# A two-block transformer kernel: x in column halves around three weight chunks, and the first query products term by term

## What is computed

```python
def rmsnorm(x, g):
    y = xf * lax.rsqrt(jnp.mean(xf * xf, axis=-1, keepdims=True) + EPS)
    return (y * g.astype(jnp.float32)).astype(x.dtype)

def retention_layer(h, g_norm, w_in, gn_gain, w_out):
    proj = rmsnorm(h, g_norm) @ w_in
    q, k, v, gate = jnp.split(proj, [...], axis=-1)
    q = rotary(heads(q, RET_QK_DIM), pos)
    k = rotary(heads(k, RET_QK_DIM), pos) * (RET_QK_DIM ** -0.5)
    ...
```

## Time and profile before

| | |
|---|---|
| median of three runs | 870.59 us |
| profiled execution | 870.52 us |
| its span (first to last instruction) | 868.7 us |
| PE busy | 857.9 us (99%) |
| DVE busy | 604.3 us (70%) |
| ACT busy | 500.8 us (58%) |
| mean bandwidth of DMA | 178 GB/s |

### The profile page before, as it was taken

The page is one execution under the profiler, slowest core; times in us unless marked ns, Lnnn a source line. Parts: engine busy times, 40 slices in busy tenths (PEclk is TensorE's granted clock), DMA queues, the critical chain, the costliest instruction groups (busy, mean ns, idle before and its releaser), DMA issues.

```text
span 868.7 us, 12207 instructions
## 1 busy us (share of the span) xinstructions
PE 857.9 (99%) x4656; PEld 732.6 (84%) x4656; DVE 604.3 (70%) x1068; ACT 500.8 (58%) x873; POOL 36.1 (4%) x49
## 2 busy tenths in 40 slices
PE   9999999999999999999999999999999999999996
PEld 8998888888899999978888788888888887888885
DVE  5986666655767875769686566788459538777674
ACT  6434544446655675958778457654535447756530
POOL 0000000000010000000000001100020000000002
PEclk9999999999999999999999999999999999999999
DMA  8764544552584877443333457574764527534511
GB/s 317 284 213 175 194 147 144 206 193 98 195 266 144 278 239 222 147 146 97 118 125 98 146 194 224 187 263 137 261 205 156 172 97 245 191 123 168 172 71 49
DMA packets 86808, 154.36 MB, mean 178 GB/s; under 512 B 3744, under 2 KB 24352, under 8 KB 86752
## 3 DMA queue, kind: packets, MB, share of 16 engines
q1 hardware_dynamic: 85248, 149.19, 51.1%
q0 software_dynamic: 1360, 4.33, 1.8%
q10 hardware_dynamic: 144, 0.07, 0.0%
HBM read 152.53 MB, written 1.05 MB: 177 GB/s over the span
## 4 chain that ended last, share of the span: by engine, by line
PE 88%; DVE 7%; ACT 2%; issue 1%; DMA 1%; POOL 0%; SPq 0%; DVEq 0%; POOLq 0%; ACTq 0%
PE acc L2236 10%; PE acc L2238 10%; PE acc L2237 10%; PE acc L2210 9%; PE acc L2212 9%; PE acc L2211 9%; PE acc L2245 4%; PE acc L2247 4%; PE acc L2246 4%; PE acc L2251 3%; PE misc L2275 2%; PE misc L2405 2%; DVE wboth L1453 2%; PE acc L2252 2%; PE acc L2265 1%
## 5 line engine op out<-in xcount | busy, mean ns | idle before, releaser
L1453 DVE TENSOR_TENSOR wboth<-raw,wboth 128x1024 fp32r<-128x1024 f32 (+1 forms) x280 | 326.2, 1213 | 55.9 <-ACT wboth L970 54.3
L970 ACT ACTIVATE wboth<-raw 128x1024 fp32r<-128x1024 f32 (+1 forms) x280 | 279.0, 1051 | 121.1 <-PE acc L2238 73.6
L2236 PE MATMUL acc<-wboth,xhiA 128*128 128x512 f32 x272 | 107.8, 396 | 0.0
L2238 PE MATMUL acc<-wboth,xloA 128*128 128x512 f32 x272 | 106.1, 390 | 0.0
L2237 PE MATMUL acc<-wboth,xhiA 128*128 128x512 f32 x272 | 106.0, 390 | 0.0
L2210 PE MATMUL acc<-wboth,xhiA 128*128 128x512 f32 x240 | 93.9, 391 | 0.0
L2212 PE MATMUL acc<-wboth,xloA 128*128 128x512 f32 x240 | 93.5, 389 | 0.0
L2211 PE MATMUL acc<-wboth,xhiA 128*128 128x512 f32 x240 | 93.4, 389 | 0.0
L2251 PE MATMUL acc<-xC,wboth 128*128 128x512 f32 x192 | 68.6, 398 | 0.0
L2236 PEld LDWEIGHTS acc<-wboth,xhiA 128*128 128x128 f32 x272 | 51.1, 188 | 11.5 <-issue 1.2
L2238 PEld LDWEIGHTS acc<-wboth,xloA 128*128 128x128 f32 x272 | 51.0, 188 | 10.8
(11 more groups left out here) (329 smaller groups left out, 1736.7 us busy)
## 6 DMA issues: line engine op xcount, KB each, us to landing
raw<-in_w_in_dram SPq DMA_DIRECT2D x36, 1024.0 KB, 5.3
raw<-in_ret_w_in_dram SPq DMA_DIRECT2D x22, 1024.0 KB, 5.2
raw<-in_nsa_w_in_dram SPq DMA_DIRECT2D x16, 1024.0 KB, 5.4
raw<-in_kv_w_dram SPq DMA_DIRECT2D x12, 1024.0 KB, 5.8
raw<-in_ret_w_out_dram SPq DMA_DIRECT2D x8, 1024.0 KB, 5.0
raw<-in_ple_w_gate_dram SPq DMA_DIRECT2D x8, 1024.0 KB, 5.1
raw<-in_nsa_w_out_dram SPq DMA_DIRECT2D x8, 1024.0 KB, 5.1
raw<-in_cmp_w_k_dram SPq DMA_DIRECT2D x4, 1024.0 KB, 5.5
```

Of the source, the lines that this page charges most:

```text
L970: nc.scalar.activation(to_hi, src, ACT.Copy).then_inc(hi_done, 1)
L1453: nc.vector.tensor_tensor(to_lo, src, to_hi.bitcast(F32), ALU.subtract).then_inc(lo_done, 1)
L2236: nc.tensor.matmul(o, xh, hi[:, j, off:off + cols], start=start, stop=False)
L2238: ins = nc.tensor.matmul(o, xl, hi[:, j, off:off + cols], start=False, stop=stop)
```

## The change

x is loaded as four DMAs: columns 0 to 511 of both tiles first, then chunks 0, 1 and 2, then columns 512 to 1023 of both tiles, then the other chunks. Accordingly PE transposes only k-tiles 0 to 3 at first; k-tiles 4 and 5 are transposed after the products of chunks 0 and 1, k-tiles 6 and 7 after those of chunk 2. ACT may take each of the first four tiles as soon as it is done (semaphore `first_columns_made`). The products of `ret_q0` are issued by term: for a k-tile the four of hi by xhi, then four of hi by xlo, then four of lo by xhi, each set with a wait of its own. There are three products of ones ahead of x's transposes where there were four, and none behind them where there was one. DVE makes chunk 5's remainder between its two `norm_stats`, where it made it after the roots were spread.

```diff
-WARM = (4, 1)
+WARM = 3
...
-    norm("ret")
+    m("norm", "ret", 0)
+    r("ret_q0", [0, 1])
+    m("norm", "ret", 1)
+    r("ret_q0", [2])
+    m("norm", "ret", 2)
+    m("norm", "ret", 3)
+    r("ret_q0", [3, 4])
     for i in range(2):
-        r(f"ret_q{i}")
         if i == 0:
             m("roots")
+        else:
+            r(f"ret_q{i}")
         r(f"ret_k{i}")
...
         @block.sync
             for m in range(MT):
-                sp.dma_start(h[:, m], w["x"][0, m * P:m * P + P]).then_inc(x_in[m], 16)
+                sp.dma_start(h[:, m, 0:HALF], w["x"][0, m * P:m * P + P, 0:HALF]).then_inc(x_in[m], 16)
             for c, (key, src, ks, width, *_) in enumerate(plan.chunks):
...
+                if c == 2:
+                    for m in range(MT):
+                        sp.dma_start(h[:, m, HALF:], w["x"][0, m * P:m * P + P, HALF:]).then_inc(x_rest_in[m], 16)
...
             def first_norm_hi():
                 for k in range(KD):
-                    misc_wait(act, "norm", "ret", k % 4)
-                    if k >= 4:
-
-                        act.wait_ge(operand_ready, xt_no["norm", "ret", k - 4] + 1)
+                    if k < 4:
+                        act.wait_ge(first_columns_made, k + 1)
+                    else:
+                        misc_wait(act, "norm", "ret", k % 4)
...
             first_norm_lo()
             norm_stats("ret", 0)
+            split_until(len(FIRST_CUTS))
             asked = norm_stats("ret", 1)
...
+            def first_queries(i, first, last):
...
+                pe.wait_ge(hi_done, plan.pieces_upto[c] + 1)
+                for j, k in enumerate(ks):
...
+                    pe.wait_ge(operand_hi_done, xt_no["norm", "ret", k] + 1)
+                    for f, (o, wh, wl) in enumerate(slices):
+                        nc.tensor.matmul(o, wh, xh, start=first and j == 0 and f % 2 == 0, stop=False,
+                                         skip_group_check=True)
+                    pe.wait_ge(operand_ready, xt_no["norm", "ret", k] + 1)
+                    for o, wh, wl in slices:
+                        nc.tensor.matmul(o, wh, xl, start=False, stop=False, skip_group_check=True)
+                    if j == 0:
+                        pe.wait_ge(lo_done, plan.pieces_upto[c + 1])
+                    for o, wh, wl in slices:
+                        ins = nc.tensor.matmul(o, wl, xh, start=False, stop=last and j == len(ks) - 1,
+                                               skip_group_check=True)
+                ins.then_inc(chunk_used, 1)
...
                         if j == 0:
                             pe.wait_ge(head_in, 16)
-                            for m, ks in ((0, (0, 4, 1, 5, 2)), (1, (0, 4)), (0, (6, 3, 7)), (1, (1, 5, 2, 6, 3, 7))):
+                            for m, ks in ((0, (0, 1, 2)), (1, (0, 1)), (0, (3,)), (1, (2, 3))):
                                 pe.wait_ge(x_in[m], 16)
                                 for k in ks:
...
+                        elif j < 3:
+                            for k in (2 * j + 2, 2 * j + 3):
+
+                                pe.wait_ge(operand_ready, xt_no["norm", "ret", k - 4] + 1)
+                                for m in range(MT):
+                                    pe.wait_ge(x_rest_in[m], 16)
+                                    ins = first_transpose(m, k)
+                                ins.then_inc(misc_full[k % 4], 1)
...
-                    if step[1] == ("norm", "ret", 3):
-                        ones_products(WARM[1])
```

More of the change, by code:

```diff
@@ L668, in build @@
         x_in = [sem(f"x_in{i}") for i in range(MT)]
+        x_rest_in = [sem(f"x_rest_in{i}") for i in range(MT)]
+        first_columns_made = sem("first_columns_made")
         const_in = sem("const_in")
@@ L1043, in _ @@
                 act.wait_ge(x_in[m], 16)
+                act.wait_ge(x_rest_in[m], 16)
                 for nb in range(2):
@@ L2170, in last_rows @@
                 return nc.tensor.matmul(o, xl, hi[:, j, at], start=False, stop=stop)
+            def first_queries(i, first, last):
+                blk = plan.blocks["ret_q0"]
+                key, _, ks, width, *_ = blk["chunks"][i]
+                c = plan.chunk_no[key]
+                ps = pair("ret_q0")
+                n = len(ks) * width
+                hi = whi[plan.slot[c]][:, 0:n].rearrange("p (k n) -> p k n", n=width)
+                lo = wlo[plan.slot[c]][:, 0:n].rearrange("p (k n) -> p k n", n=width)
+                pe.wait_ge(hi_done, plan.pieces_upto[c] + 1)
+                for j, k in enumerate(ks):
+                    xh, xl = operand(blk, k, 0, T)
+                    slices = [(ps[f // 2][:, (f % 2) * T:(f % 2) * T + T], hi[:, j, f * P:f * P + P],
+                               lo[:, j, f * P:f * P + P]) for f in range(4)]
+                    pe.wait_ge(operand_hi_done, xt_no["norm", "ret", k] + 1)
[11 more added lines that the diff above has]
+                ins.then_inc(chunk_used, 1)
             def chunk(name, i, first, last, part=None, rows=False):
+                if name == "ret_q0":
+                    first_queries(i, first, last)
+                    return
                 blk = plan.blocks[name]
@@ L2276, in transposes, with first_transpose @@
                 return ins
+            def first_transpose(m, k):
+                return nc.tensor.transpose(first_columns(k)[:, m * P:m * P + P], h[:, m, k * P:k * P + P], ident)
             def misc(name):
@@ L2290, in misc @@
                             pe.wait_ge(head_in, 16)
-                            for m, ks in ((0, (0, 4, 1, 5, 2)), (1, (0, 4)), (0, (6, 3, 7)), (1, (1, 5, 2, 6, 3, 7))):
+                            for m, ks in ((0, (0, 1, 2)), (1, (0, 1)), (0, (3,)), (1, (2, 3))):
                                 pe.wait_ge(x_in[m], 16)
                                 for k in ks:
[L2294 to L2297, removed]
+                                    ins = first_transpose(m, k)
+                                    if m:
+                                        ins.then_inc(first_columns_made, 1)
+                        elif j < 3:
[3 more added lines that the diff above has]
+                                    pe.wait_ge(x_rest_in[m], 16)
+                                    ins = first_transpose(m, k)
+                                ins.then_inc(misc_full[k % 4], 1)
                         return
@@ L2481, in _ @@
             pe.wait_ge(warm_set, 1)
-            ones_products(WARM[0])
+            ones_products(WARM)
             for step in plan.sched:
```

## The result

| | before | after |
|---|---|---|
| median of 15 runs | 870.74 us | 872.91 us |
| lowest to highest | 870.37 to 871.00 | 871.24 to 876.10 |
| profiled execution | 870.52 us | 872.28 us |
| its span | 868.7 us | 870.5 us |

The ratio is 1.0026, with a 95% interval from 1.0019 to 1.0033: slower by 0.26%. The forecast was 871.1 (869.2 to 872.6), "no difference that counts". The loss is 2.17 us, four times the 0.55 that I forecast. The spread is as telling as the median: the kernel before repeats within 0.6 us, the change doesn't.

What follows compares the result with a forecast made beforehand. PE, busy 99% of the span, bounds the kernel; only the start of `ret_k0` moves: 6.45 + 15.0 = 21.45 against 20.88, +0.55 us, so 871.1 us (8 in 10: 869.2 to 872.6; own range 870.4 to 871.9).

Steps and rivals of the forecast that it cites:

- The two chains that meet at `ret_k0`: At the start of `ret_k0`: PE's own products and ACT's path to the roots meet; the second decided, at 20.88 us.
- the start comes forward: First product of `ret_q0`: needs only ACT's halves, so it starts at 6.45 us instead of 8.36.
- the roots go back: ACT's path to `roots`: tile 6 taken at 13.2, 1.3 us later, so the spread ends at 20.95 instead of 19.68.
- tile 6's transposes are the link: On PE, transposes of k-tiles 6 and 7 stand behind 48 products, so ACT gets tile 6 1.3 us later.
- chunk 5's remainder off the path: On DVE, made during ACT's second pair of squares; wins the time between `roots` and `ret_k0` except 0.43 us.
- the order by terms free: Products of `ret_q0`: 12 per k-tile before and after, 0.12 us each, added waits met, so no cost to PE.
- a wait of about 2 us ahead of `roots`: On PE, products done at 18.9, spread ending at 20.95: PE stands idle for 2.1 us.
- K - P: P is the start of the first product, K that of `ret_k0`; forecast as K = P + 15.0 us.
- landings go by bytes: DMA landings at the start follow bytes moved: x's second half by about 4.7 (second tile's first columns), chunk 3 at 10.3.
- x's second half: DMA of x's later columns, ahead of chunk 3: lands by about 9, PE asks at 9.35, so hidden.
- rival 3: DMA late: x's second half or chunk 3 lands 2 us later, K +1.5 to +2, 872.3 us; chance 0.05.
- Rival 1: PE's clock rises late: first products at half pace for 4.3 us, losing 2.1, total +2.7, 873.3 us; chance 0.12.

Runs made afterwards that it cites:

- experiment 6: The change with the transposes of k-tiles 6 and 7 ahead of chunk 2's products instead of behind them: median 870.72 us, ratio 1.0003.
- experiment 8: The kernel before with only chunk 5's remainder moved ahead of the second `norm_stats`: 870.18 us, ratio 0.9996.
- experiment 4: The change with four products of ones ahead of x's transposes, one behind the first eight, and four in the wait ahead of `roots`: median 871.53 us, ratio 1.0011.
- experiment 1: The change itself run again, nothing altered, for a second profile: median 872.91 us, profiled execution 874.52, ratio 1.0025 against the kernel before.
- experiments 2 and 4: The first of them: the change with four products of ones ahead of x's transposes and one behind the first eight, median 871.99 us; the other is experiment 4.
- experiment 5: The kernel before with DVE making the remainders of chunks 5 and 6 ahead of the second `norm_stats`: 873.13 to 876.29 us, ratio 1.0050.

## Why the prediction was wrong

**What held.** The two chains that meet at `ret_k0`; that the start comes forward and the roots go back; that tile 6's transposes are the link (experiment 6); chunk 5's remainder off the path (experiment 8: 0.44 us); the order by terms free (12 products in 1.44 us before and after); a wait of about 2 us ahead of `roots` (1.97 measured); nothing new behind `ret_k0` in the profiled execution. K - P was 14.92 against my 15.0 where PE didn't wait for x (experiment 4), and with its two idle places filled the change measured 871.53, inside the forecast's own range. In the profile of the change K - P was 15.77, for the reason that follows.

**First fault, a size: "landings go by bytes".** Head came as worked out (transposes from 4.15), but x's second tile at 5.3 and not 4.7, so P was 6.83 and not 6.45. x's second half landed at 10.66 and not "by about 9", which was to be hidden; the transposes of tiles 4 and 5 waited until 10.70. These two make K 22.60 instead of 21.45: +1.72 instead of +0.55. The step took the amount moved by each moment from the kernel before and assumed that the change would move as much; it moved 2.66 MB for 3.00. Chunk 3 landed at 12.0 and not at 10.3, which stayed hidden. The late landings were in rival 3, at 0.05.

**Second fault, a mechanism under-priced and one place of it missed.** Rival 1 had the half pace at the start with a chance of 0.12. I wrote against it that "three ones and eight transposes still fill most of the time"; in the profile of experiment 1 they didn't fill enough. The length was nearly right: half pace for 4.1 us from the first product against my 4.3. But it made K only 0.75 later than in the first profile, and not 2.1, since the slower products partly replaced the wait for x's second half. The second place I had in my own working and did not price: "stands idle for 2.1 us" appears as a harmless by-product of the late roots, yet it is where the pace falls behind `roots`, 1.5 us in experiment 1. My working gave it nothing. Of 23 runs of the change, 9 lie from 871.1 to 871.8, 7 from 872.3 to 873.5 and 7 at 874.1 and above. Only two of them were profiled. The granted clock over the whole run speaks to the later drop: 0.998 or 0.999 in the nine lowest and in the 872.28, 0.995 to 0.997 in the thirteen others. A single 0.997 decides nothing, since the kernel before reads 0.997 in a few runs too, and half pace at the start isn't in this figure where no rise had been recorded before it.

So the median of 872.91 is the kernel before plus about 0.9 for the late roots (experiment 4) and 1.4 for the two drops and the late landing of x's second half together, taking medians; how the 1.4 divides isn't shown. My own range ended at 872.6 because I had given the clock one place and one chance in eight.

The Trainium skill (TensorE: Matmul & The Clock Gate, Part 1) says that the throttled state is the default and activity releases it. The trace agrees, in both directions: pace doubled at 10.7, after products since 6.64, and halved at 24.4, behind a wait, in one execution. Whether transposes count less than products, the rule I had weighed, no run here shows, since experiments 2 and 4 add products and no other load.

## What to carry to other kernels

Work that only fills PE's time can be worth its microsecond: before removing ones products, or accepting a wait "that costs nothing because it is on no path", look for steps between matmuls of the same form, and price the half pace that may follow it. When a producer's step is moved behind a consumer's work on an in-order engine, follow every other user of that step: here the sums of squares, three steps further on ACT, paid for operand tiles that PE delivered late. And a time that spreads where it didn't before is a finding: take a second profile before explaining the first.

## What the runs showed that I had not expected

A wait of 1.97 us was enough for PE's pace to halve 1.3 us after its end, for 3.4 us (experiment 1); the mild profile of the change had a wait of 1.97 as well and kept its pace. So the same program falls or doesn't, from run to run. With 2.85 us of waiting, three runs of four fell (experiment 5: one by its profile, two by their times and granted clocks). The granted clock shows 1.00 for a half-paced stretch at the program's start, as long as no change of level has been recorded, and 0.50 for one later on; steps between equal matmuls show both.
